# Query tiles in front of forget tiles, with one sigmoid table for both

## What is computed

```python
q = jax.nn.silu(q_raw)                                   # silu(x) = x * sigmoid(x)
logf = jnp.log(lb + (1.0 - lb) * jax.nn.sigmoid(f_raw))
k = (1.0 - lb) * jax.nn.sigmoid(-f_raw)
b = cumsum(logf)                                         # within a chunk of 64
decay = exp(b_t - b_s)                                   # for s <= t
A = einsum('td,tsd,sd->ts', q, decay, k)
out = inter(q * exp(b), S) + A @ v                       # then a norm, times silu(z)
```

## Time and profile before

| | us |
|---|---|
| median of 3 runs | 1629.01 (1626.87 to 1635.09) |
| the profiled execution, its own time | 1628.98 |
| span of its trace, first to last instruction | 1627.2 |
| TensorE busy | 1579.5 (97%) |
| VectorE busy | 1151.1 (71%) |
| ScalarE busy | 861.8 (53%) |
| GpSimd busy | 139.8 (9%) |

### The profile page before, as it was taken

The page is one execution under the profiler, slowest core; times in us unless marked ns, Lnnn a source line. Parts: engine busy times, 40 slices in busy tenths (PEclk is TensorE's granted clock), DMA queues, the critical chain, the costliest instruction groups (busy, mean ns, idle before and its releaser), DMA issues.

```text
span 1627.2 us, 24289 instructions
## 1 busy us (share of the span) xinstructions
PE 1579.5 (97%) x9650; PEld 1404.5 (86%) x9650; DVE 1151.1 (71%) x1696; ACT 861.8 (53%) x1321; POOL 139.8 (9%) x164
## 2 busy tenths in 40 slices
PE   8999999988999999898999999999999999999999
PEld 6787889987999999886789888888888888888887
DVE  6888868877678976656677777777777777555544
ACT  6766446677655555454556554444444444444442
POOL 0000000312120320031414000000000000000000
PEclk9999999999999999999999999999999999999999
DMA  9999975513557864432234445555555545555552
GB/s 377 354 357 372 375 263 208 207 66 132 190 178 261 322 226 156 148 137 78 104 130 156 169 177 198 185 188 197 198 175 197 199 175 196 207 184 204 183 205 104
DMA packets 47825, 331.02 MB, mean 203 GB/s; under 512 B 5281, under 2 KB 6689, under 8 KB 8417
## 3 DMA queue, kind: packets, MB, share of 16 engines
q1 hardware_dynamic: 45184, 312.20, 52.4%
q0 software_dynamic: 2240, 17.04, 2.7%
q10 hardware_dynamic: 290, 0.25, 0.1%
HBM read 327.37 MB, written 2.10 MB: 202 GB/s over the span
## 4 chain that ended last, share of the span: by engine, by line
PE 71%; DVE 14%; ACT 6%; issue 3%; DMA 3%; POOL 2%; SPq 0%; ACTq 0%; DVEq 0%; POOLq 0%
PE ps L1142 19%; PE ps L1143 10%; PE ps L1138 6%; PE ps L1140 6%; PE ps L1139 6%; DVE wl L1886 5%; PE ps L1195 5%; PE ps L1197 5%; PE ps L1196 5%; DVE raw L1932 3%; ACT wh L1488 3%; DMA raw<-in_wts 2%; DMA xs<-in_xN 1%; PE ps L1185 1%; PE ps L1186 1%
## 5 line engine op out<-in xcount | busy, mean ns | idle before, releaser
L1886 DVE TENSOR_TENSOR wl<-raw,wh 128x1024 fp32r<-128x1024 f32 x512 | 624.0, 1232 | 346.9 <-ACT wh L1488 346.6
L1488 ACT ACTIVATE wh<-raw 128x1024 fp32r<-128x1024 f32 x512 | 531.4, 1055 | 357.3 <-PE ps L1197 130.5
L1142 PE MATMUL ps<-hA,wh 128*128 128x512 f32 x1408 | 488.7, 390 | 0.0
L1143 PE MATMUL ps<-hA,wl 128*128 128x256 f32 x1408 | 397.0, 282 | 0.0
L1142 PEld LDWEIGHTS ps<-hA,wh 128*128 128x128 f32 x1408 | 264.3, 188 | 55.3
L1143 PEld LDWEIGHTS ps<-hA,wl 128*128 128x128 f32 x1408 | 266.1, 189 | 0.0
L1138 PE MATMUL ps<-hA,wh 128*128 128x256 f32 x752 | 220.6, 293 | 0.0
L1139 PE MATMUL ps<-hA,wh 128*128 128x256 f32 x752 | 212.5, 283 | 0.0
L1140 PE MATMUL ps<-hA,wl 128*128 128x256 f32 x752 | 212.4, 282 | 0.0
L1138 PE MATMUL ps<-hB,wh 128*128 128x256 f32 x576 | 167.1, 290 | 5.7 <-issue 2.4
L1139 PE MATMUL ps<-hB,wh 128*128 128x256 f32 x576 | 162.9, 283 | 0.0
(11 more groups left out here) (287 smaller groups left out, 2065.2 us busy)
## 6 DMA issues: line engine op xcount, KB each, us to landing
raw<-in_wts SPq DMA_DIRECT2D x256, 1024.0 KB, 4.8
raw<-in_ada SPq DMA_DIRECT2D x36, 1024.0 KB, 5.6
side<-in_ada POOLq DMA_DIRECT2D x12, 1024.0 KB, 9.9
work<-in_memN SPq DMA_DIRECT2D x2, 1024.0 KB, 8.9
xs<-in_xN POOLq DMA_DIRECT2D x1, 2048.0 KB, 20.6
xs<-in_xT POOLq DMA_DIRECT2D x2, 1024.0 KB, 6.3
out_rows<-xs SPq DMA_DIRECT2D x8, 256.0 KB, 2.5
wp<-in_dt SPq DMA_DIRECT2D x8, 128.0 KB, 2.6
```

The source lines that it names most:

```text
L1142: e.matmul(ps[bank][:, :], w1, hl, start=first, stop=False)
L1143: i = e.matmul(ps[bank][:, T:2 * T], w2, hl[:, 0:T], start=False, stop=last)
L1488: e.activation(wh[:, h % WS, :], raw[:, n % RAW, part * HALF:(part + 1) * HALF], ACT.Copy).then_inc(s_hi)
L1886: e.tensor_tensor(wl[:, h % WS, :], src, wh[:, h % WS, :].bitcast(F32), ALU.subtract).then_inc(s_lo)
```

## The change

- `MIX`: q stands in front of f in every pair. The gate pages that used to be loaded with q are loaded with f, at the same place in the list.
- q has no eviction of its own. When f is complete, ScalarE takes three sigmoids straight from PSUM, one of q and two of f, between two table loads. `fin` is not filled any more; the head of the recursion loses its first step.
- VectorE multiplies the sigmoid of q with q in PSUM.
- The planner's costs are changed with it (f 4.5 and 0.65, q none), and what waited for the silu of q now waits for the multiply.

```diff
-MIX = (("f", 0), ("q", 0), ("f", 1), ("q", 1), ("z", 0), ("z", 1), ("f", 2), ("q", 2), ...
+MIX = (("q", 0), ("f", 0), ("q", 1), ("f", 1), ("z", 0), ("z", 1), ("q", 2), ("f", 2), ...
-REC_HEAD = ("sigmoid", "gk", "ln", "scan", "d12", "x1", "x2")
+REC_HEAD = ("gk", "ln", "scan", "d12", "x1", "x2")
-EVAC_COST = dict(f=(0.63, 0), q=(3.2, 0), z=(1.9, 0), ...
+EVAC_COST = dict(f=(4.5, 0.65), z=(1.9, 0), ...
...
+    for n in range(4):
+        o.hooks["q", 2 * n + 1] = lambda tile: None
...
+            if tile[0] == "q":
+                return after(("f", tile[1]), "dve", "q")
...
-                    e.wait_ge(*after(("q", 2 * pr + 1), "act", "ev"))
+                    e.wait_ge(*after(("f", 2 * pr + 1), "dve", "q"))
...
-                if k == "sigmoid":
-                    e.wait_ge(*after(("f", 2 * pr + 1), "act", "ev"))
-                    e.activation(kk, f, ACT.Sigmoid, scale=-1.0).then_inc(mark(t, "act", "kk"))
-                    e.activation(E, f, ACT.Sigmoid).then_inc(mark(t, "act", "E"))
-                    e.preload_act_table_set("natural_log_exp_and_others")
...
+                    if name == "f":
+                        e.wait_ge(*tile_end(("q", j)))
+                        e.activation(qin[:, pr % 2, :], ps[o.banks["q", j][0]][:, :], ACT.Sigmoid).then_inc(mark(t, "act", "q"))
+                        e.activation(kks[pr % 2], src, ACT.Sigmoid, scale=-1.0).then_inc(mark(t, "act", "kk"))
+                        e.activation(Es[pr % 2][1], src, ACT.Sigmoid).then_inc(mark(t, "act", "ev"))
+                        e.preload_act_table_set("natural_log_exp_and_others")
+                        return
...
+                if name == "f":
+                    q = qin[:, j // 2 % 2, :]
+                    e.wait_ge(*after(t, "act", "q"))
+                    e.tensor_tensor(q, q, ps[o.banks["q", j][0]][:, :], ALU.mult).then_inc(mark(t, "dve", "q"))
```

More of the change, by code:

```diff
@@ L65 @@
 SOFTMAX = ("scores", "max", "exp", "rc", "scale", "turn", "pt", "pv")
[L66 removed]
+MIX = (("q", 0), ("f", 0), ("q", 1), ("f", 1), ("z", 0), ("z", 1), ("q", 2), ("f", 2), ("q", 3), ("f", 3), ("z", 2), ("z", 3), ("az", 0), ("az", 1), ("az", 2), ("az", 3))
 MIX_COLS = {"f": 5120, "q": 4096, "z": 7168, "az": 3072}
[L68 removed]
+GATES_WITH = {("f", 0), ("f", 1), ("z", 1), ("f", 2), ("az", 1), ("f", 3), ("z", 3), ("az", 3)}
 GATES_AT = range(4, 12)
[L70 removed]
+REC_HEAD = ("gk", "ln", "scan", "d12", "x1", "x2")
 REC = ("f1", 1, 2, 3, 4, 5, 6, "copies", "l7", "cross", "at", "pv")
@@ L84 @@
     qn=dict(s0="a.65", **{f"s{n}": "a.65|d.6" for n in range(1, 8)}, s8="d.6", r1="d.2", rstd="a.4", r4="d.6"),
-    rf={"sigmoid": "a3.9", "gk": "d2.1", "ln": "a.65", "scan": "d1.8", "d12": "o4.2", "x1": "a.65", "x2": "a.65"},
+    rf={"gk": "d2.1", "ln": "a.65", "scan": "d1.8", "d12": "o4.2", "x1": "a.65", "x2": "a.65"},
     rec={"f1": "o.8|p.85|d.9 o2.1",
@@ L100 @@
 )
-EVAC_COST = dict(f=(0.63, 0), q=(3.2, 0), z=(1.9, 0), az=(1.9, 0), un=(0.42, 0), uq=(0.42, 0), ur=(0.42, 0), lq=(0.42, 0.45), lkv=(0.42, 0.45),
+EVAC_COST = dict(f=(4.5, 0.65), z=(1.9, 0), az=(1.9, 0), un=(0.42, 0), uq=(0.42, 0), ur=(0.42, 0), lq=(0.42, 0.45), lkv=(0.42, 0.45),
                  kr=(0, 0.45), mq=(0, 0.45), pz=(0, 0.9), wo=(0, 0.48), oa=(0, 0.45), ob=(0, 0.45), o2=(0, 0.45), uv=(1.3, 0))
@@ L108 @@
 WIDE_TILES = ("g", "u")
-ACT_TILES = ("f", "q", "z", "az", "un", "uq", "ur")
+ACT_TILES = ("f", "z", "az", "un", "uq", "ur")
 RMS_TILES = ("lq", "lkv", "kr", "mq", "pz")
@@ L1805, in act_tile @@
                 e.wait_ge(*tile_end(t))
-                if name in ("f", "q", "z"):
+                if name in ("f", "z"):
                     pr = j // 2
@@ L1811, in act_tile @@
                         e.wait_ge(*after(("part", 2), "dve", 3))
-                    dst, src = {"f": fin, "q": qin, "z": zin}[name][:, pr % 2, :], ps[o.banks[t][0]][:, :]
+                    dst, src = zin[:, pr % 2, :], ps[o.banks[t][0]][:, :]
+                    if name == "f":
[5 more added lines that the diff above has]
+                        return
                 elif name == "az":
@@ L1826, in act_tile @@
                         e.wait_ge(*after(("mla", 2 * (j - 2) + 1), "pe", "s"))
-                e.activation(dst, src, ACT.Silu if name in ("q", "z", "az") else ACT.Copy).then_inc(mark(t, "act", "ev"))
-                if name == "q" or (name == "z" and j % 4 == 3) or (name == "az" and j % 4 == 2):
+                e.activation(dst, src, ACT.Silu if name in ("z", "az") else ACT.Copy).then_inc(mark(t, "act", "ev"))
+                if (name == "z" and j % 4 == 3) or (name == "az" and j % 4 == 2):
                     e.preload_act_table_set("natural_log_exp_and_others")
@@ L1981, in rec_head @@
                 if k == "gk":
-                    e.wait_ge(*after(t, "act", "E"))
+                    e.wait_ge(*after(("f", 2 * pr + 1), "act", "ev"))
                     if pr == 0:
```

## The result

| | us |
|---|---|
| before, median of 11 runs beside it | 1631.58 (1626.87 to 1636.54) |
| after, median of 11 runs | 1638.94 (1635.47 to 1642.86) |
| ratio after / before | 1.0046, 95% interval 1.0036 to 1.0057 |
| the profiled execution of after, its own time | 1640.53 |
| span of its trace | 1638.7 |

What follows compares the result with a forecast made beforehand. TensorE, busy for 97% of the span, was taken as the bound, its own work plus gaps. Terms 4.7 + 0.8 + 0.5 + 0.8 = +6.8 us on 1629 gave 1636 us, range 1627 to 1642.

Steps and rivals of the forecast that it cites:

- stretch A: Stretch without projection matmuls ahead of pair 2's f tiles, 326 to 342 us before; forecast from near 320 to near 349.
- ScalarE's saving: Two table loads and the copy of f fewer in each of four pairs: 12.7 us of ScalarE, hidden by matmuls.
- VectorE's multiply: Four multiplies of 128x512 with one operand in PSUM, 0.68 us each, 2.7 us in all, costing TensorE 0.
- Rival 4: Slower by VectorE's queue: the multiply holds up the weights' low halves and TensorE waits for them; 1644 us, chance 0.05.
- A begins earlier: Last projection matmul ahead of stretch A out near 320.4 us instead of 326.1, 5.7 us earlier.
- The level-7 product 12.0 us later: In stretch A, the recursion's last cross level comes 12.0 us behind the last projection matmul, where before it was 3.4.
- From there 11.5 us: From the level-7 product to the first projection matmul of the new group: 11.5 us, where before it was 12.7.
- 5.4 to the second level: From TensorE's resumed projection behind stretch A to the next recursion's second level: 5.4 us, where before it was 2.4.
- B +0.8: Stretch ahead of pair 3's f tiles: recursion waits go, -4.0; uncovered eviction ahead of scores adds 4.8 idle; net +0.8 us.
- half a spell more: Longer stretch A has room for a second half-clock spell costing up to 1.7 us; half of that, +0.8.
- rival 3: Slower by the clock: gaps of the longer stretch A bring two half-clock spells, not half of one; 1641 us, chance 0.23.
- 4.7 + 0.5 + 0.8: Next recursion's second level 4.7 us later; 0.5 more idle between the two stretches; 0.8 for half-clock time in stretch A.

Runs made afterwards that it cites:

- the run with the evictions alone: Kernel before, its order and plan kept, with f emptied by two sigmoids from PSUM and q by a sigmoid and VectorE's multiply: 1629.5 us, ratio 1.0007.
- the run with the norm ahead: Changed kernel with recursion 0's norm and recursion 1's first level put ahead of the maxima and exponents of heads 2 and 3: 1638.34 us, 1.0037 to before.
- the four traces of A: Changed kernel profiled twice unchanged (1.0046, 1.0063), and with useless matmuls where TensorE waits, 88 (1.0029) or 44 (1.0072); A lasts 27.1 to 27.8 us.

## Why the prediction was right, and where it was not

The time (1636 against 1638.9 at the median) and the sign came out, and so did the mechanism: a late head, a longer stretch A, a wait for VectorE handed on to the next recursion. That the sum is so close is luck, as the last paragraph of this section shows. By its steps:

- **ScalarE's saving, VectorE's multiply: right.** 12.6 and 3.0 us, where 12.7 and 2.7 stood; the run with the evictions alone shows that both are hidden. Rival 4 fell with it: nobody waits for the multiply, and the low halves never hold TensorE.
- **A begins earlier: right.** The first profile of after entered the stage 1.8 us later than before did, so that goes off its times; the second 0.1. The last projection matmul is then at 319.9 in both, where 320.4 stood.
- **The level-7 product 12.0 us later: wrong by 3.3.** It is 15.5 and 15.2. I began the walk with ScalarE's table load right behind the last projection matmul. It stood at 325.07, 3.3 us behind it:

```profile
320.70 0.82 POOL L2405 TENSOR_TENSOR E<-early 128x256 f32<-128x256 f32 x1
321.60 0.68 POOL L2407 TENSOR_TENSOR E<-early 128x256 f32<-128x256 f32 x1
```

```profile
322.31 0.63 ACT L1572 ACTIVATE E<-E 128x512 f32<-128x512 f32 x1 [1.02 <-POOL E L2407]
322.84 1.04 ACT L1492 ACTIVATE wh<-raw 128x1024 fp32r<-128x1024 f32 x1
323.79 1.26 ACT L1639 ACTIVATE xs<-xs,cols 128x128 f32<-128x128 f32 x4
325.07 1.28 ACT L1833 ACT_TABLE_LOAD   x1
```

  The head of recursion 1 is late too. GpSimd's decays of it end at 322.28, ScalarE's exponent waits for them, and behind it queue a split, four scalings and then the table load. VectorE's low half of that split and its own scalings follow on it:

```profile
323.92 1.22 DVE L1892 TENSOR_TENSOR wl<-raw,wh 128x1024 fp32r<-128x1024 f32 x1 [2.11 <-ACT wh L1492]
325.06 0.87 DVE L2108 TENSOR_SCALAR xs<-xs,cols 128x128 f32<-128x128 f32 x4
```

  The transposes need the scalings of both engines, and VectorE's end last. That is the wait of 2.67 us that the profile could only call "issue". I had written of GpSimd's decays that they change places by a few rows and carry the same work. They do; but ScalarE waits for them in the order of its queue. Everything behind, to the level-7 product, is late by about the same 3.3. This is read from the rows; no run moved the decays to test it.
- **From there 11.5 us, then 5.4 to the second level, 4 of them a wait: right.** 12.4 and 11.7, 5.2 and 5.2, wait 3.93 and 3.92. The share of the maxima in that wait was overrated: 1.0 us of it, by the run with the norm ahead.
- **B +0.8: wrong, it is -2.5.** The wait is 3.38 us and not 4.8, because the table load ran ahead. That is 1.4 of the 3.3 us. The rest lies in what went away: the waits of B cost 5.0 us in the ledger of before, where I had taken 4.0, and the matmuls between them follow each other 1.1 us closer in after. I had read in the order that the load itself waits for a finished tile; the wait that it carries was met before this tile's end. The waits for the recursion went as forecast.
- **The rest.** The clock was put at 0.8 us with half a spell more; it is some 17 us more at half clock and 2 us, perhaps more. In rival 3 I had priced a fall at half its length; in a stretch that waits for others it costs a quarter of that.

In the ledger: A and what it hands on were forecast at 4.7 + 0.5 + 0.8 = +6.0 and measure +9.5; B was forecast at +0.8 and measures -2.5; the rest +0.5. The sum of 6.8 against 7.5 is as good as it is because two errors of 3.5 and 3.3 us stand against each other. The sign did not hang on that.

## What to carry to other kernels

An edit that saves work on an engine with slack is worth what it does to the order: ask first which result it delays, and who collects that delay at a place with nothing to cover it. Walk such a place from what is still queued on every engine at its start, the slow ones' leftovers too, not from an empty queue. And before a clock spell is priced, look at what bounds the stretch it falls on.

## What was unexpected of the hardware

- **A half clock costs little where TensorE waits.** 0.13 us for a microsecond in A of after, 0.44 in the dense work of before. The first comes from one pair of profiles; the four traces of A say the same.
- **GpSimd's own work got longer.** 57 instructions in the stage in either kernel, 50.0 and 47.0 us in the two profiles of before, 60.0 in both of after. One subtraction of 128x256 takes 0.61 to 0.65 us when VectorE is idle (the last two rows), and up to 2.83 us beside some of its instructions. VectorE and GpSimd in the same time, with VectorE idle from 321.81 to 323.92:

```profile
314.69 2.29 DVE L1938 CUSTOM_DVE_ANT_0 raw<-raw,work 128x2048 f32<-128x2048 f32 x1
...
317.15 2.99 DVE L1892 TENSOR_TENSOR wl<-raw,wh 128x1024 fp32r<-128x1024 f32 x2
```

```profile
314.69 2.83 POOL L2407 TENSOR_TENSOR early<-early 128x256 f32<-128x256 f32 x1
317.59 1.47 POOL L2405 TENSOR_TENSOR work<-early 128x256 f32<-128x256 f32 x1
319.14 1.48 POOL L2407 TENSOR_TENSOR work<-early 128x256 f32<-128x256 f32 x1
...
322.35 0.61 POOL L2405 TENSOR_TENSOR work<-early 128x256 f32<-128x256 f32 x1
323.05 0.65 POOL L2407 TENSOR_TENSOR work<-early 128x256 f32<-128x256 f32 x1
```

  That the two hold each other up is what the lengths suggest, since in after the four of over 2.5 us in the stage all stand beside VectorE's L1938, and none that stands by itself is over 0.65; no run here took VectorE's work away to show it. It lengthens just the chain that delays A.
